# Summing the conditioning partitions by adding DMAs in DRAM, in a twelve-block transformer kernel

## The reference

```
mod = silu(c) @ ada_w[l] + ada_b[l]          # 1024 x 6144, six rows of 1024
shift1, scale1, gate1, shift2, scale2, gate2 = mod
h = norm(x) * gain * (1 + scale) + shift     # ahead of mixer (1) and feed-forward (2)
x = x + gate * branch(h)
```

## Time and profile before

| | |
|---|---|
| median of three runs | 2203.25 us |
| the profiled execution's own time | 2201.21 us |
| its span, first to last instruction | 2199.4 us |
| TensorE busy | 2135.6 us, 13639 matmuls and transposes |
| weight loads of TensorE (beside the matmuls) | 1901.6 us |
| VectorE busy | 1569.0 us |
| ScalarE busy | 1080.3 us |
| GpSimd busy | 204.6 us |
| moved by DMA | 472.47 MB, 215 GB/s on average |
| granted TensorE clock, mean | 0.995 |

### The profile page before, as it was taken

How to read it: one execution, slowest core, us unless ns; L and a number is a source line. 1 busy time by engine, 2 the same in 40 slices (tenths; PEclk the granted TensorE clock), 3 DMA queues, 4 the chain that set the end, 5 groups by cost and what they waited for, 6 DMA issues and landing times. The chain is left out here.

```text
span 2199.4 us, 34071 instructions
## 1 busy us (share of the span) xinstructions
PE 2135.6 (97%) x13639; PEld 1901.6 (86%) x13639; DVE 1569.0 (71%) x2168; ACT 1080.3 (49%) x2087; POOL 204.6 (9%) x242
## 2 busy tenths in 40 slices
PE   8999999999999999999999998999999999999998
PEld 7999888879988888777999787899898899778997
DVE  6578657766775677667899677899745896657545
ACT  5454555544545464455445543454555454464433
POOL 1101001101010011010001001001000001111000
PEclk9999999999999999999999999999999999999999
DMA  9988645577785455534899534799644797525561
GB/s 306 291 259 251 221 138 159 181 239 221 251 278 186 139 167 198 199 125 129 302 348 360 163 114 143 247 360 363 214 135 138 242 358 251 184 80 174 198 206 74
DMA packets 297284, 472.47 MB, mean 215 GB/s; under 512 B 20241, under 2 KB 153051, under 8 KB 297126
## 3 DMA queue, kind: packets, MB, share of 16 engines
q1 hardware_dynamic: 286566, 440.68, 60.1%
q0 software_dynamic: 10560, 29.61, 4.5%
HBM read 465.36 MB, written 4.85 MB: 214 GB/s over the span
## 5 line engine op out<-in xcount | busy, mean ns | idle before, releaser
L150 DVE TENSOR_TENSOR wlo<-raw,whi 128x1024 fp32r<-128x1024 f32 x640 | 774.6, 1238 | 202.5 <-ACT whi L144 200.6
L144 ACT ACTIVATE whi<-raw 128x1024 fp32r<-128x1024 f32 x640 | 648.6, 1057 | 161.3 <-DMA raw<-in_ffn_w_gu 69.9
L138 PE MATMUL G<-HTh,whi 128*128 128x256 f32 x2336 | 671.4, 287 | 9.4 <-ACT pool L144 7.0
L138 PE MATMUL G<-HTh,wlo 128*128 128x256 f32 x2336 | 661.7, 283 | 0.0
L138 PE MATMUL G<-HTl,whi 128*128 128x256 f32 x2336 | 661.5, 283 | 0.0
L138 PEld LDWEIGHTS G<-HTh,whi 128*128 128x128 f32 x2336 | 448.5, 192 | 18.2 <-issue 10.6
L138 PEld LDWEIGHTS G<-HTl,whi 128*128 128x128 f32 x2336 | 448.7, 192 | 2.1
L138 PEld LDWEIGHTS G<-HTh,wlo 128*128 128x128 f32 x2336 | 448.4, 192 | 0.0
L144 ACT ACTIVATE pool<-G 128x128 f32<-128x128 f32 (+2 forms) x400 | 165.5, 434 | 529.8 <-PE G L138 472.0
L138 PE MATMUL G<-whi,HTh 128*128 128x512 f32 (+1 forms) x784 | 312.9, 399 | 20.3 <-ACT HTh L144 11.1
L138 PE MATMUL G<-whi,HTl 128*128 128x512 f32 (+1 forms) x784 | 303.7, 387 | 4.2 <-DVE HTl L158 4.1
(11 more groups left out here) (194 smaller groups left out, 2267.4 us busy)
## 6 DMA issues: line engine op xcount, KB each, us to landing
raw<-in_ada_w SPq DMA_DIRECT2D x192, 512.0 KB, 6.2
raw<-in_ffn_w_gu SPq DMA_DIRECT2D x352, 256.0 KB, 5.0
raw<-in_w_in SPq DMA_DIRECT2D x128, 512.0 KB, 4.6
raw<-in_ffn_w_down SPq DMA_DIRECT2D x88, 512.0 KB, 7.0
raw<-in_w_in SPq DMA_DIRECT2D x160, 256.0 KB, 4.5
raw<-in_swa_w_in SPq DMA_DIRECT2D x24, 512.0 KB, 4.6
pool<-mod_rows POOLq DMA_DIRECT2D x24, 512.0 KB, 6.3
raw<-in_gla_w_in SPq DMA_DIRECT2D x24, 512.0 KB, 5.4
```

The source lines that it names most:

```text
L138: return self.e.matmul(out, a, b, start=start, stop=stop, skip_group_check=True) if self.e else self
L144: return self.e.activation(out, a, func, bias=bias, scale=scale, accum_out=accum) if self.e else self
L150: return self.e.tensor_tensor(out, a, b, op) if self.e else self
```

## The change

The sums over the partitions are taken by DMAs in DRAM. SyncE stores each unit's accumulator (128 x 512) to a scratch mod_parts, 8 pieces behind its last one (ada_out, called from fetch). Four units make a group of 2048 columns, three groups a layer. Four steps after a group's last store, GpSimd issues the first of five adding DMAs: rows 64 to 127 are added to rows 0 to 63, then 32 rows to 32, 16, 8 and 4, three steps apart, each waiting for the one before. What is left are 4 rows of 2048. Nineteen steps after the store, mod_load loads them, the bias and, where a scale is in the group, the norm's gain, to 16 partitions; four steps later VectorE sums the five rows (h_mod) and forms gain * (1 + scale), and GpSimd stores the result to mod_rows. The row loads stay, but wait for their group, not for the whole layer. ada_sums, mod_rows, h_ada_tr, h_ada_sum, h_ada_mod, h_mod_T and h_amod go, with the tiles adb and mod; the bias and gains are no longer loaded and transposed in setup. The pool has 46 blocks in place of 44. For one matmul of the gated linear attention, gemm asks for two free banks instead of three.

```diff
-NB = 44
+NB = 46
+    def dma_add(self, out, a):
+        return self.e.dma_start(out, a, accum_op=ALU.add, max_dma_last_dim=4096) if self.e else self
...
+        self.part = nc.dram_tensor("mod_parts", (4, 3, P, 2 * D), F32, kind="Internal").ap()
...
         self.h_piece(r, segs, i, self.raw_free[r])
+        while self.adaq and self.adaq[0][4] <= i - NRAW:
+            self.ada_out(*self.adaq.pop(0)[:4])
...
         if k == 0:
-            self.acc = self.mk_blk(2)
+            self.acc = self.blk(2)
...
         if k == 3:
-            self.adaq.append((l, u, self.acc, done, self.steps))
+            self.adaq.append((l, u, self.acc, done, p.i))
...
+    def ada_out(self, l, u, b, acc):
+
+        n, part = 12 * l + u, self.M.part[l, u // 4][:, u % 4 * 512:u % 4 * 512 + 512]
+        wrote = (f"part{n % 4}", n)
+        before = [(f"part{n % 4}", n - 4)] if n > 3 else []
+        self.h_load("SP", wrote, part, b.a, [acc] + before)
+        b.release([wrote])
+        self.wrote.append(wrote)
+        if u % 4 == 3:
+            src, self.wrote = self.wrote, []
+            for k in range(5):
+                self.soon.append([4 + 3 * k, lambda k=k: self.fold(l, u // 4, k, src)])
+            self.soon.append([19, lambda: self.mod_load(l, u // 4)])
+
+    def fold(self, l, g, k, src):
+
+        part, h = self.M.part[l, g], 64 >> k
+        self.h_add((f"half{(3 * l + g) % 2}", (l, g, k)), part[0:h, :], part[h:2 * h, :], [(f"half{(3 * l + g) % 2}", (l, g, k - 1))] if k else src)
+
+    def mod_load(self, l, g):
+
+        M, b = self.M, self.mk_blk(4)
+        parts = b.a[0:16, 0:640].rearrange("a (r p) -> a r p", p=P)
+        gain, scaled = b.a[0:16, 768:896], b.a[0:16, 896:1024]
...
+        self.h_load("POOL", (name, (n, 0)), parts[:, 4, :], bias, b.w)
+        if g != 1:
...
+            self.h_load("POOL", (name, (n, 1)), gain, gains, b.w)
+        ready = [(name, (n, 2))]
+        self.h_load("POOL", ready[0], parts[:, 0:4, :], M.part[l, g][0:4, :].rearrange("r (a p) -> a r p", p=P),
+                    b.w + [(f"half{n % 2}", (l, g, 4))])
+
+        def made():
...
+            self.h_mod(b.a[0:16, 640:768], parts.rearrange("a r p -> a p r"), gain, scaled, ready, summed, done, g != 1)
...
+            self.h_load("POOL", evs[0], M.mrows[l][16 * g:16 * g + 16], b.a[0:16, 640:768], [summed])
+            if g != 1:
+                self.h_load("POOL", evs[1], M.mrows[l][48 + 4 * g:56 + 4 * g], scaled[8 - 4 * g:16 - 4 * g, :], [done])
...
+        self.soon.append([4, made])
...
-            self.advance(lambda: self.gheld.count(False) > 2)
+            self.advance(lambda: self.gheld.count(False) > (1 if key[0] == "gla" and key[2] == 5 else 2))
...
-            if kk == 2:
-                self.ada_sums(4, 0)
...
-            if kk == 4 and self.modq and not all(self.gheld):
-                self.mod_rows()
...
-        self.ada_sums(2)
...
-        tab = [self.load("SP", f"ab{i}", ab[i].a[0:96, 0:P], abv[96 * i:96 * i + 96, :]) for i in range(2)]
...
+    def h_mod(self, m, parts, gain, scaled, ready, summed, done, scale):
+        e = self.e
+        for x in ready:
+            e.wait_ge(*self.at(x))
+        e.tensor_reduce(m, parts, ALU.add).then_inc(*self.up(summed))
+        if not scale:
+            return
+        e.wait_ge(*self.at(summed))
+        e.scalar_tensor_tensor(scaled, m, 1.0, gain, ALU.add, ALU.mult).then_inc(*self.up(done))
...
+    def h_add(self, ev, dst, src, waits):
+        for t in waits:
+            self.e.wait_ge(*self.at(t))
+        self.e.dma_add(dst, src).then_inc(*self.up(ev, 16))
```

More of the change, by code:

```diff
@@ L455, in h_none @@
         pass
-    h_load = h_memset = h_piece = h_split = h_rest = h_ada = h_ada_tr = h_ada_sum = h_ada_mod = h_mm = h_mm1 = h_none
+    h_load = h_memset = h_piece = h_split = h_rest = h_ada = h_add = h_mod = h_mm = h_mm1 = h_none
     h_copy = h_silu = h_tanh = h_gate = h_square = h_rstd = h_mean = h_pow = h_rows = h_none
     h_tr = h_affine = h_split_tr = h_cols = h_lam = h_btab = h_bias = h_addx = h_resid = h_none
-    h_mod_T = h_spread = h_mean2 = h_by = h_xa = h_gu0 = h_gu0_tr = h_amod = h_narrow = h_rope = h_kvT = h_none
+    h_spread = h_mean2 = h_by = h_xa = h_gu0 = h_gu0_tr = h_narrow = h_rope = h_kvT = h_none
     h_gu = h_down = h_down1 = h_last_gain = h_last_rows = h_end = h_none
@@ L781, in give @@
         self.spl_free[n % NSPL] = [used]
[L783 to L804, removed]
@@ new lines, in fold @@
+    def fold(self, l, g, k, src):
[5 more added lines that the diff above has]
+        gain, scaled = b.a[0:16, 768:896], b.a[0:16, 896:1024]
+        n, bias = 3 * l + g, M.I["ada_b_2"][l].rearrange("(a p) -> a p", p=P)[16 * g:16 * g + 16, :]
+        name = f"rows{n % 2}"
+        self.h_load("POOL", (name, (n, 0)), parts[:, 4, :], bias, b.w)
+        if g != 1:
+            gains = M.I["norm_gain_2"][l][g // 2].rearrange("(a p) -> a p", p=P).unsqueeze(0).to_broadcast([2, 8, P])
+            self.h_load("POOL", (name, (n, 1)), gain, gains, b.w)
[3 more added lines that the diff above has]
+        def made():
+            summed, done = ("ve_mod", (l, g, 0)), ("ve_mod", (l, g, 1))
+            self.h_mod(b.a[0:16, 640:768], parts.rearrange("a r p -> a p r"), gain, scaled, ready, summed, done, g != 1)
+            evs = [(f"mod{n % 2}", (n, k)) for k in range(2 if g != 1 else 1)]
+            self.h_load("POOL", evs[0], M.mrows[l][16 * g:16 * g + 16], b.a[0:16, 640:768], [summed])
+            if g != 1:
+                self.h_load("POOL", evs[1], M.mrows[l][48 + 4 * g:56 + 4 * g], scaled[8 - 4 * g:16 - 4 * g, :], [done])
+            for c in {0: (0, 8, 48), 1: (16, 24), 2: (32, 40, 56)}[g]:
+                self.mod_ev[l, c] = evs[-1]
+            b.release(evs[-1:])
+        self.soon.append([4, made])
@@ L2189, in h_mm1 @@
         mm.then_inc(*self.up(done))
-    def h_ada_tr(self, g, b, acc, free, summed):
-        e, M = self.e, self.M
-        for t in free:
-            e.wait_ge(*self.at(t))
-        e.wait_ge(*self.at(acc))
-        e.wait_ge(*self.at(self.tid))
-        for n in range(4):
-            mm = e.transpose(M.GB[g][:, n * P:n * P + P], b.a[:, n * P:n * P + P], M.ident[:, :])
-        mm.then_inc(*self.up(summed))
     def h_tr(self, g, src, ready, free, tr):
@@ L2231, in h_cols @@
             e.wait_ge(*self.at(t))
-        e.transpose(M.GB[g][:, 0:P], vr, M.ident[:, :])
-        for i in range(2):
-            mm = e.transpose(M.GB[g2][:, 96 * i:96 * i + 96], ab[i].a[0:96, 0:P], M.ident[0:96, 0:96])
-        mm.then_inc(*self.up(trs))
+        e.transpose(M.GB[g][:, 0:P], vr, M.ident[:, :]).then_inc(*self.up(trs))
     def h_btab(self, g, rbt, oh, dmk, btb, ready, tdm, mm, done):
@@ L2241, in h_btab @@
         e.matmul(M.GB[g][0:20, :], rbt, oh, True, True).then_inc(*self.up(mm))
-    def h_mod_T(self, g, b, l, free, ready, tr, have):
-        e, M = self.e, self.M
-        for t in free + [ready, self.tid]:
-            e.wait_ge(*self.at(t))
-        e.transpose(M.GB[g][0:64, 0:P], M.mod[:, 64 * l:64 * l + 64], M.ident[:, :]).then_inc(*self.up(tr))
     def h_kvT(self, g, t, kvb, ready, kT, free, tr, done):
@@ L2727, in h_dil @@
             self.round_head(u, 4 + u["h"])
-    def h_ada_sum(self, g, b, summed, added, tot):
-        e = self.e
-        e.wait_ge(*self.at(summed))
-        for n in range(4):
-            c = slice(n * P, n * P + P)
-            op = e.activation(b.a[:, c], self.M.GB[g][:, c], ACT.Copy, accum=tot[:, n:n + 1])
-        op.then_inc(*self.up(added))
     def h_identr(self, tid, done):
```

69 lines of the change are left out of this document (14 added, 55 removed).

## The result

The changed kernel takes 2242.09 us in the median (2239.61 to 2246.16, 4 runs), the kernel before 2203.19 beside it (2202.01 to 2206.47, 4 runs). The ratio is 1.0177, 95% interval 1.0165 to 1.0189. The forecast was 2196 us with a range of 2182 to 2213, so it was wrong in sign and by 46 us. The profiled execution took 2241.46 us, its span is 2239.7.

A forecast was written before the change was run, and what follows sets the result against it. TensorE's instructions were taken to set the time, with DMA engines full in feed-forward layers 0 to 2. Terms -7.0 - 0.2 + 1.8 - 0.5 - 0.4 - 0.5 made -6.8 us: median 2196 us, range 2182 to 2213.

The forecast's parts named there:

- queues: SyncE and GpSimd issue lists: GpSimd's added DMAs cost 62 us of issue on an engine 9% busy, nothing in the sum.
- rival 3: Late rows hold VectorE or GpSimd at the turns, some 4 us at each of two: 2204 us, chance 0.10.
- the plan's relaid lists: Whole kernel: lists laid out anew by the planner, taken as 0, a few us each way left to the range.
- The transposes: TensorE, 48 groups at 0.44 us, 21.1 us: 7.0 first-kind layers, 5.3 each feed-forward layers 0 and 1, 3.5 layer 2.
- The DMA time that comes: Feed-forward layers 0 to 2: stores and folds load full DMA engines, leaving net -0.2, +1.8 and -0.5 us.
- The factor of about two for a fold's bytes: Adding DMAs: each costs twice the time of moving its bytes once, as source and destination are read.
- rival 1: Feed-forward stretches: folds cost their bytes once, DMA work is hidden, transposes' time stays won: 2183 us, chance 0.30.
- the stock of halves: Feed-forward layers 0 to 2: TensorE draws on weight halves made ahead, counted as 6, 6 and 3 us.
- the main step: Feed-forward DMA supply: wrong if DMA share rises with OTl spacing still 17.0 us, or if spacing is over 18.
- under 8.6: First fold of a group in the DMA issues: lands in under 8.6 us by the forecast, more by the slower rival.
- SyncE's shorter start: Start of kernel: three small loads ahead of the first weights go, 0 to 1.2 us, taken as 0.5 gained.
- The slower rival: Feed-forward stretches: a fold costs three times its bytes or more, weights come late: 2210 us, chance 0.22.

The follow-up runs named there:

- D: Changed kernel without stores and folds, four rows of weights standing for the sums, its lists in the same order: 2215.65 us, 1.0050 to the kernel before.
- J: D with the row stores 10 weight steps later in GpSimd's list: 2186.57 us, 0.9928 to the kernel before.
- after: The changed kernel, complete, as first measured: 2242.09 us, 1.0177 to the kernel before.
- H: Complete changed kernel with one edit, the stores of finished rows 10 weight steps later in GpSimd's list: 2223.83 us, 1.0088 to the kernel before.
- F: Changed kernel with nothing behind VectorE's partial sums (no stores, folds, row loads, VectorE sum or row stores): 2184.26 us, 0.9911 to the kernel before.
- E: Kernel before, own lists, without its 192 transposes of partial sums, ScalarE's sums replaced by 48 small copies: 2189.39 us, 0.9932 to the kernel before.
- I: H with an own tile for row loads and folds from feed-forward stretches kept until the next mixer's tables are loaded: 2196.71 us, 0.9966.
- A: Changed kernel without the 60 folds, stores and everything else kept in order: 2221.06 us, 1.0073 to the kernel before.
- K: Changed kernel with folds unchained on their own scratch, same bytes, and row stores 10 weight steps later: 2223.94 us, 1.0094 to the kernel before.

## Why the prediction was wrong, step by step

- **"GpSimd gains 60 adding DMAs, 32 loads and 20 stores at about 0.55 us of issue each, 62 us, on an engine that is 9% busy"** (queues) is the step that failed most. It put GpSimd's new waits into the sum at nothing. The place of the row stores alone costs 29 us (D against J), 18 of them still to be had with the DMAs in (after against H). I had written that the bias loads stand behind GpSimd's waits, and sent them to rival 3; there I priced only the turns, at 4 us each. The mistake was to price instructions at 0.55 us of issue, and not to ask for each new wait what is behind it and how far ahead of its use that was. The earlier trace rows show the store of mod_rows once per layer, at 619.3 us for the first; in the change it comes three times a layer, in front of the bias loads. The 0 that I took for the plan's relaid lists was right: F has them and is 5 us faster than E.
- **Rival 3, late rows at the turns,** was right in that waits on GpSimd's list cost time at the first turn, and too small: 13.5 us against 4. Behind the waits stand the decay table and the gate loads, which I had not named. Its sign, VectorE waiting for the loads from mod_parts, is not in the trace; it was GpSimd that waited for VectorE. The second turn, between FF layer 1 and the next mixer, shows no such jump.
- **The transposes, -21.1 us.** E measured -14.7. By stretch 6.6 came in the first-kind layers (7.0 forecast) and 5.1 in FF layer 0 (5.3), so the 0.44 us per group nearly holds (6.6 / 16 = 0.41). FF layer 1 gave 3.5 instead of 5.3, and layer 2 lost 1.5 instead of gaining 3.5, with no DMA added: from 1735 to 1812 us E's TensorE waited 4.4 us for wlo, at a DMA share of 1.02, where the kernel before waited for nothing. A TensorE that is ahead meets its weights before they come.
- **The DMA time that comes.** I had the three stretches give the transposes' gain back up to -0.2, +1.8 and -0.5 us. In H, where the lists are clean of row stores, they are +5.1 (halves 296 to 360), +6.8 and +4.6. So stores and folds there are worth 24 us over E against my 15, and the folds alone as much, by H against I. The rate was right, 380 GB/s against 379 over whole stretches (I), and the 358 GB/s of the Trainium skill ("DMA: Bandwidth & Descriptors", section "Where 436 GB/s comes from") are passed there over 145 us. The factor of about two for a fold's bytes fits too: in the changed kernel's 1060 to 1260 us, queue q0 took 9.0% of the engines for 4.29 MB, and q1 85.8% for 60.50. If the 1.57 MB of row loads on q0 cost per MB what q1's do, the folds took 1.7 times as much per MB (an estimate), and not once, as rival 1 had it. What was too kind is the stock of halves that I let run down, 6, 6 and 3 us. Without it my three sums are +5.8, +7.8 and +2.5, together 16.1, and H has 16.5. That is arithmetic; no run changed the stock. ScalarE's waits for the gate and up weights grew from 69.9 to 116.0 us over the kernel. GpSimd's OTl, whose spacing I had named as the sign (17.6 us by the forecast, over 18 and the main step is wrong), is 17.9 us apart over six units and 18.7 over eight:

```profile
1069.78 1.29 POOL L150 TENSOR_TENSOR OTl<-pool,OTh 128x512 fp32r<-128x512 f32 x1 [24.15 <-ACT OTh L144]
...
1177.10 1.85 POOL L150 TENSOR_TENSOR OTl<-pool,OTh 128x512 fp32r<-128x512 f32 x1 [10.05 <-ACT OTh L144]
...
1219.02 1.30 POOL L150 TENSOR_TENSOR OTl<-pool,OTh 128x512 fp32r<-128x512 f32 x1 [11.17 <-ACT OTh L144]
```

- **Sizes.** The first fold landed in 8.4 us, within my "under 8.6". The reduction took 1.31 us instead of 0.8 and an adding DMA's issue 0.8 instead of 0.55; neither shows in the time. SyncE's shorter start gave nothing: half 0 starts 1.3 us later than before in after, but also 1.0 later in E, whose start is unchanged.
- **The slower rival** (fold three times its bytes, 2210) had the right sign. Its three stretches make +14.3, near H's 16.5, but by luck: a fold took 1.7 times its bytes, not three. All of it would have explained 14 of the 46 us missed.

In sum, from 2189.4 (E) to 2242.1, by the table: 17 us at the two first-kind jumps, 13.5 at the turn, 9.5 and 8.7 in FF layers 0 and 1, 3.4 in layer 2 and 1.4 behind it.

What stays open: why the stores cost time in A and not in I, what makes the rest of the turn's loss in K, and how much could still be had from a last mixer where the folds stand behind the rope additions, which wasn't tried.

## What to carry to other kernels

Before a DMA that waits for another engine is put into an in-order queue, list what is behind it there and how early that used to go out. The wait's price is that lead lost, not the issue time, and moving the instruction ten steps back can be the whole fix, as in J. Traffic that isn't urgent belongs into the stretches where the DMA engines are half idle: the folds of eight groups (8 MB) cost some 24 us and a turn's wait in the full stretches of H, and in the mixers of I nothing that shows in two of them, and 8 us in the last, where they stood in front of other work. When a prediction's gain is gone, run the change with all its work left out and only its waits kept; that separated list from bytes here in one run (D).

## What the runs showed of the hardware

- TensorE's clock fell at the new gaps. At the turn of the changed kernel it was granted 0.50 (1.2 GHz) from 1272 to 1282 us, behind an idle gap of 7.51 us, and the same behind the gaps of 5.93 and 6.61 us at the other two jumps. The kernel before has no such gap there and was granted 1.00 (2.4 GHz) at the place of the turn. Three windows of the changed kernel, then one of the kernel before:

```profile
249.50:254.50 5.00, 4.99 (x14) 4.12 (x15) 4.05 (x5) 0.89 (x3) 1.42 (x2) 0.50 0.69 176
686.60:691.40 4.80, 4.80 (x11) 3.79 (x12) 4.71 (x6) 0.60 (x1) 0.70 (x1) 0.50 0.79 183
1272.00:1282.00 10.00, 9.60 (x31) 7.08 (x32) 3.46 (x5) 5.88 (x7) 3.21 (x5) 0.50 0.19 33
...
1236.00:1252.00 16.00, 15.70 (x95) 12.15 (x94) 8.74 (x12) 6.61 (x10) 1.71 (x4) 1.00 0.79 278
```

The first instructions behind the turn's gap, grouped, of the changed kernel and then of the kernel before:

```profile
L138 PE MATMUL G<-pool 16*128 16x512 f32 x4 | 3.8, 1089 | 7.5 <-issue 7.5
```

```profile
L138 PE MATMUL G<-pool 16*128 16x512 f32 x4 | 2.0, 614 | 0.0
```

A gap thus costs more than its length. For the first jump the account closes: 5.93 us of gap, 2.5 for 5 us of work at half the clock, less the 0.5 that E gains there, is 7.9, and the jump is 8.0 (at the second 6.61 + 2.4 - 0.5 = 8.5, against 8.7).
- The landing of an adding DMA from DRAM to DRAM follows its size only weakly: 16 times the bytes land in about twice the time (count, KB, us to landing, the changed kernel):

```profile
mod_parts<-mod_parts POOLq DMA_DIRECT2D x12, 512.0 KB, 8.4
mod_parts<-mod_parts POOLq DMA_DIRECT2D x12, 256.0 KB, 6.9
mod_parts<-mod_parts POOLq DMA_DIRECT2D x12, 128.0 KB, 5.6
mod_parts<-mod_parts POOLq DMA_DIRECT2D x12, 64.0 KB, 4.3
mod_parts<-mod_parts POOLq DMA_DIRECT2D x12, 32.0 KB, 3.9
mod_rows<-pool POOLq DMA_DIRECT2D x12, 8.0 KB, 2.4
```

So a chain of five is 29 us long (8.4 + 6.9 + 5.6 + 4.3 + 3.9), though the last two move 96 KB.
- The 256 KB stores from SBUF in I's first two full stretches (7.5 us to landing, DMA share 1.05 and 1.06) took nothing from TensorE that shows. A against D says that this is no rule.
